# Differential attention scores: two maps as 64-row matmul pairs on the two row groups, three products of parts, pieces of 512 columns

## What is computed

```python
s = einsum('ibhqd,ibhkd->ibhqk', qblk, k) * scale + bias   # i: the map, 0 or 1
s = where(rel >= 0, s, -inf)                               # causal
p = softmax(s, axis=-1)
a = p[0] - lam * p[1]
o = einsum('bhqk,bhkd->bhqd', a, v)
```

## Time and profile before

| | |
|---|---|
| median of 3 runs | 2482.14 us |
| lowest to highest | 2478.25 to 2485.72 us |
| span of the profiled execution | 2482.5 us |
| PE busy | 2290.3 us, 92% |
| DVE, ACT, POOL busy | 56%, 49%, 31% |
| mean granted clock of TensorE | 0.968 |

### The profile page before, as it was taken

How to read it: one execution, slowest core, us unless ns; L and a number is a source line. 1 busy time by engine, 2 the same in 40 slices (tenths; PEclk the granted TensorE clock), 3 DMA queues, 4 the chain that set the end, 5 groups by cost and what they waited for, 6 DMA issues and landing times. The chain is left out here.

```text
span 2482.5 us, 36835 instructions
## 1 busy us (share of the span) xinstructions
PE 2290.3 (92%) x11480; PEld 1838.1 (74%) x11480; DVE 1382.3 (56%) x2806; ACT 1207.9 (49%) x1639; POOL 766.9 (31%) x686
## 2 busy tenths in 40 slices
PE   6999999997999999999979996699999999999980
PEld 5788889996777667766658885577888888788760
DVE  6321221104777777777546776676655565666663
ACT  5111111113777677767644443475554555656653
POOL 0000000003887778777600111222222222222220
PEclk9999999998999999999989997799999999999995
DMA  5433334224553454344036444599877878988957
GB/s 196 161 120 126 114 131 121 62 65 121 134 126 81 100 134 100 81 100 132 18 133 206 133 129 162 203 334 353 285 263 250 273 241 279 314 288 282 325 148 288
DMA packets 207632, 441.51 MB, mean 178 GB/s; under 512 B 19081, under 2 KB 56113, under 8 KB 205490
## 3 DMA queue, kind: packets, MB, share of 16 engines
q1 hardware_dynamic: 188530, 379.46, 46.1%
q0 software_dynamic: 19008, 60.91, 9.8%
HBM read 338.55 MB, written 101.76 MB: 177 GB/s over the span
## 5 line engine op out<-in xcount | busy, mean ns | idle before, releaser
L1495 DVE TENSOR_TENSOR gu_lo<-gu_raw,gu_hi 128x2048 fp32r<-128x2048 f32 x128 | 293.2, 2291 | 124.2 <-issue 86.8
L622 POOL TENSOR_TENSOR p_ring<-p_ring 128x512 f32<-128x512 f32 (+2 forms) x192 | 334.2, 1741 | 16.0
L682 DVE TENSOR_SCALAR_CACHE_REDUCE p_ring<-ps_s 128x512 f32<-128x512 f32 (+6 forms) x352 | 277.0, 791 | 101.6 <-PE ps_s L753 94.3
L647 ACT ACTIVATE p_ring<-p_ring,shift 128x1152 f32<-128x1152 f32 (+15 forms) x256 | 305.8, 1197 | 22.5 <-DVE shift L698 22.5
L790 PE MATMUL ps_o<-aT,v_st 128*128 128x512 f32 (+3 forms) x640 | 285.5, 530 | 0.0
L636 ACT ACTIVATE aT<-ps_t 128x512 f32<-128x512 f32 (+1 forms) x320 | 168.8, 530 | 171.4 <-PE ps_t L775 170.2
L1435 ACT ACTIVATE gu_hi<-gu_raw 128x2048 fp32r (+1 forms) x128 | 237.9, 1915 | 9.5 <-PE ps_g L1572 4.9
L1572 PE MATMUL ps_g<-gu_hi,xT_lo 128*128 128x512 f32 x720 | 235.6, 408 | 7.5 <-DVE xT_lo L1510 7.5
L1572 PE MATMUL ps_g<-gu_lo,xT_hi 128*128 128x512 f32 x720 | 227.8, 398 | 0.0
L1572 PE MATMUL ps_g<-gu_hi,xT_hi 128*128 128x512 f32 x720 | 227.6, 397 | 0.0
L619 POOL TENSOR_SCALAR p_ring<-p_ring,coef 128x512 f32<-128x512 f32 (+2 forms) x192 | 167.7, 873 | 133.7 <-DVE coef L711 131.9
(11 more groups left out here) (217 smaller groups left out, 4358.9 us busy)
## 6 DMA issues: line engine op xcount, KB each, us to landing
gu_raw<-in_moe_w_gate SPq DMA_DIRECT2D x128, 512.0 KB, 8.6
gu_raw<-in_moe_w_up SPq DMA_DIRECT2D x128, 512.0 KB, 9.8
d_raw<-in_moe_w_down SPq DMA_DIRECT2D x64, 1024.0 KB, 7.2
qk<-stage SPq DMA_DIRECT2D x64, 512.0 KB, 2.8
q_first<-qk SPq DMA_DIRECT2D x64, 256.0 KB, 5.0
q_second<-qk SPq DMA_DIRECT2D x64, 256.0 KB, 5.1
w_raw<-in_diff_w_in POOLq DMA_DIRECT2D x12, 1024.0 KB, 6.6
k<-qk SPq DMA_DIRECT2D x8, 1024.0 KB, 12.5
```

Of the source, the lines that this page charges most:

```text
L622: pool.tensor_tensor(p0(r, c0, c1), p0(r, c0, c1), p1(r, c0, c1), ALU.add).then_inc(mixed, 1)
L647: nc.scalar.activation(p, p, ACT.Exp, bias=shift[:, r % 8, m:m + 1], accum_out=sums[:, r % 8, m:m + 1]).then_inc(raised, 1)
L682: ins = nc.vector.tensor_scalar(p(r, k0, k0 + far), ps_s[:, c % 2, 0:far], SCALE, None, ALU.mult, ALU.max, accum_out=top[:, r % 4, m, col: ...
L1495: nc.vector.tensor_tensor(gu_lo[:, j * GC:(j + 1) * GC], raw(half, j), gu_hi[:, j * GC:(j + 1) * GC].bitcast(F32), ALU.subtract).then_inc( ...
```

## The change

- The two maps of a piece are scored together. q's place now holds, for each part, both maps under each other (map 0 in partitions 0 to 63, map 1 in 64 to 127), and k's too. A matmul takes the 64 rows of one map. The six matmuls of a pair of pieces go in the order (low q, high k), (high q, low k), (high q, high k), each for map 0 and then map 1. The product of the two low parts is no longer computed.
- Pieces have at most 512 columns. A row's first piece takes what is over a multiple of 512 (128, 256, 384 or 512), the rest are 512 wide. Pieces of map 0 and 1 alternate in `pieces`: 640 in place of 384, in 320 pairs.
- `ps_s` is two buffers of two maps of 512 columns (one bank each); the pair starts when DVE has taken the pair before the last (`taken >= c - 2`).
- `take` and `peaks` use up to five columns of `top` for a map.
- The loads of q and k are one DMA each; q's has half the bytes. Places in SBUF shrink, with filler tiles that keep the others where they were.
- `slots` are made by the same rule, two pieces at a time.

```diff
 def load_q_quad(eng, scratch, place, h, j, landed):
-    for hl in range(2):
-        for lanes in (slice(0, HALF), slice(HALF, P)):
-            eng.dma_start(place[lanes, hl].bitcast(F32),
-                          scratch["qk"][h, hl, :, j * 512:(j + 1) * 512].rearrange("(m d) t -> d m t", m=2)
-                          ).then_inc(landed, 16)
+    eng.dma_start(place.bitcast(F32), scratch["qk"][h, :, :, j * 512:(j + 1) * 512].rearrange("l p t -> p l t")
+                  ).then_inc(landed, 16)
...
         w = (i + 1) * P
-        for m in range(2):
-            head = WIDE // 2 if w <= 3 * WIDE // 2 else WIDE
-            for k0, n in [(0, w)] if w <= WIDE else [(0, head), (head, w - head)]:
+        k0 = 0
+        while k0 < w:
+            n = (w - k0 - 1) % PIECE + 1
+            for m in range(2):
                 pieces.append((r, m, k0, n))
+            k0 += n
...
-            scored_cost += pieces[c][3] / (2 * P)
-            c += 1
+            scored_cost += pieces[c][3] / P
+            c += 2
...
-        ps_s = ctx.enter_context(nc.psum_tensor("ps_s", [P, 2, WIDE], F32))
+        ps_s = ctx.enter_context(nc.psum_tensor("ps_s", [P, 2, 2, PIECE], F32))
...
                 if far:
-                    col = 0 if not last else 1
-                    ins = nc.vector.tensor_scalar(p(r, k0, k0 + far), ps_s[:, c % 2, 0:far], SCALE, None,
+                    col = 3 - ((i + 1) * P - k0 - n) // PIECE
+                    ins = nc.vector.tensor_scalar(p(r, k0, k0 + far), ps_s[:, c // 2 % 2, m, 0:far], SCALE, None,
                                                   ALU.mult, ALU.max, accum_out=top[:, r % 4, m, col:col + 1])
...
-                if c >= 2:
-
-                    pe.wait_ge(taken, c - 1)
+                if c >= 4:
+
+                    pe.wait_ge(taken, c - 2)
                 a = i % 4
-                for j in range(0, n, 512):
-                    e = min(512, n - j)
-                    for hl in (1, 0):
-                        mm = pe.matmul(ps_s[:, c % 2, j:j + e], q_st[g % 2][:, hl, m, a * P:(a + 1) * P],
-                                       k_st[h % 2][:, m, k0 + j:k0 + j + e], start=hl == 1, stop=hl == 0)
-                mm.then_inc(scored, 1)
+                for k, (ql, kl) in enumerate(((1, 0), (0, 1), (0, 0))):
+                    for m in range(2):
+                        lanes = slice(m * HALF, (m + 1) * HALF)
+                        mm = pe.matmul(ps_s[:, c // 2 % 2, m, 0:n], q_st[g % 2][lanes, ql, a * P:(a + 1) * P],
+                                       k_st[h % 2][lanes, kl, k0:k0 + n], start=k == 0, stop=k == 2)
+                        if k == 2:
+                            mm.then_inc(scored, 1)
...
-                for c in slots[n]:
+                for c in slots[n][::2]:
                     score(c)
```

More of the change, by code:

```diff
@@ L144, in _ @@
             sp.wait_ge(moved, 32)
-            for hl in range(2):
-                sp.dma_start(k0[hl * HALF:(hl + 1) * HALF].bitcast(F32),
-                             scratch["qk"][HEADS, hl].rearrange("(m d) t -> d m t", m=2)).then_inc(k0_in, 16)
+            sp.dma_start(k0[:, :, :].bitcast(F32), scratch["qk"][HEADS].rearrange("l p t -> p l t")).then_inc(k0_in, 16)
             def store_v(b, first):
@@ L159, in _ @@
             sp.wait_ge(filled, QK_FILLS + (VB - 1) * TILES + 1)
-            load_q_quad(sp, scratch, keep["q_first"], 0, FIRST_QUAD, sem("b_q_in0"))
+            load_q_quad(sp, scratch, keep["q_first"][:, :, :], 0, FIRST_QUAD, sem("b_q_in0"))
             sp.dma_start(keep["near_both"][:, 0, :], scratch["near"][0]).then_inc(k0_in, 16)
@@ L397, in attend @@
     WIDE = 1024
+    PIECE = 512
     QUADS = (FIRST_QUAD, 0, 3, 1)
@@ L490, in attend @@
         oT = sb("oT", [P, 512])
-        sb("q_first_place", [P, 2, 2, 512], F32R)
-        q_st = (keep["q_first"], sb("q_second", [P, 2, 2, 512], F32R))
+        sb("q_first_place", [P, 2, 512], F32R)
+        q_st = (keep["q_first"], sb("q_second", [P, 2, 512], F32R))
+        sb("w_rest_place", [P, 2, D])
         sb("near_place", [P, 2, NEAR])
@@ L495, in attend @@
         o_sb = sb("o_sb", [P, 2, 4, P])
-        top = sb("top", [P, 4, 2, 3])
+        top = sb("top", [P, 4, 2, 5])
         shift = sb("shift", [P, 8, 2])
@@ L532, in load_k @@
         def load_k(eng, h):
-            for hl in range(2):
-                eng.dma_start(k_st[h % 2][hl * HALF:(hl + 1) * HALF].bitcast(F32),
-                              scratch["qk"][HEADS + h, hl].rearrange("(m d) t -> d m t", m=2)).then_inc(k_in[h % 2], 16)
+            eng.dma_start(k_st[h % 2][:, :, :].bitcast(F32), scratch["qk"][HEADS + h].rearrange("l p t -> p l t")
+                          ).then_inc(k_in[h % 2], 16)
         def load_near(eng, h):
@@ L548, in load_q @@
             h, j = quads[g]
-            load_q_quad(eng, scratch, q_st[g % 2], h, j, q_in[g % 2])
+            load_q_quad(eng, scratch, q_st[g % 2][:, :, :], h, j, q_in[g % 2])
         @block.sync
@@ L670, in take @@
                     if r % 16 == 0:
-                        dve.wait_ge(k_in[h % 2], 48 * (h // 2 + 1))
+                        dve.wait_ge(k_in[h % 2], 32 * (h // 2 + 1))
                     if p0_frees[r] >= 0:
@@ L685, in take @@
                     ins = nc.vector.tensor_tensor_reduce(
-                        p(r, k0 + far, k0 + n), ps_s[:, c % 2, far:n], near[:, h % 2, NEAR - n_near:NEAR],
-                        SCALE, LOWEST, ALU.add, ALU.max, top[:, r % 4, m, 2:3])
+                        p(r, k0 + far, k0 + n), ps_s[:, c // 2 % 2, m, far:n], near[:, h % 2, NEAR - n_near:NEAR],
+                        SCALE, LOWEST, ALU.add, ALU.max, top[:, r % 4, m, 4:5])
                 ins.then_inc(taken, 1)
@@ L692, in peaks @@
                 i = rows[r][1]
-                first = 0 if i >= 8 else 1 if i >= 2 else 2
+                first = 4 - ((i + 1) * P + PIECE - 1) // PIECE if i >= 2 else 4
                 if r >= 8:
@@ L697, in peaks @@
                 dve.wait_ge(taken, last_piece[r] + 1)
-                nc.vector.tensor_reduce(shift[:, r % 8, :], top[:, r % 4, :, first:3], AX.X, ALU.max,
+                nc.vector.tensor_reduce(shift[:, r % 8, :], top[:, r % 4, :, first:5], AX.X, ALU.max,
                                         negate=True).then_inc(peaked, 1)
@@ L737, in score @@
             def score(c):
-                r, m, k0, n = pieces[c]
+                r, _, k0, n = pieces[c]
                 g, i = rows[r]
@@ L742, in score @@
                     if r % 16 == 0:
-                        pe.wait_ge(k_in[h % 2], 48 * (h // 2 + 1))
+                        pe.wait_ge(k_in[h % 2], 32 * (h // 2 + 1))
                     if r % 4 == 0:
-                        pe.wait_ge(q_in[g % 2], 64 * (g // 2 + 1))
-                if c >= 2:
-                    pe.wait_ge(taken, c - 1)
+                        pe.wait_ge(q_in[g % 2], 16 * (g // 2 + 1))
+                if c >= 4:
+                    pe.wait_ge(taken, c - 2)
                 a = i % 4
-                for j in range(0, n, 512):
-                    e = min(512, n - j)
-                    for hl in (1, 0):
-                        mm = pe.matmul(ps_s[:, c % 2, j:j + e], q_st[g % 2][:, hl, m, a * P:(a + 1) * P],
-                                       k_st[h % 2][:, m, k0 + j:k0 + j + e], start=hl == 1, stop=hl == 0)
-                mm.then_inc(scored, 1)
+                for k, (ql, kl) in enumerate(((1, 0), (0, 1), (0, 0))):
[5 more added lines that the diff above has]
+                            mm.then_inc(scored, 1)
             def ps_t_free(t):
@@ L1707, in build @@
         with nc.sbuf_tensor("hn_place", [P, 2, KC, SEQ], F32):
-            with nc.sbuf_tensor("q_first", [P, 2, 2, 512], F32R) as q_first:
+            with nc.sbuf_tensor("q_first", [P, 2, 512], F32R) as q_first:
                 keep["q_first"] = q_first
-                with nc.sbuf_tensor("w_place", [P, 2, D], F32):
+                with nc.sbuf_tensor("w_place", [P, 3, D], F32):
                     with nc.sbuf_tensor("near_both", [P, 2, 2 * P], F32) as near_both:
```

## The result

The changed kernel takes 2510.72 us (median of 4 runs, 2510.29 to 2512.92) against 2483.57 us before on the same chip: 1.0116 times as long, 95% interval 1.0101 to 1.013. It is 27 us slower where 35 us less was forecast. The time lies in the range given (2425 to 2560 us), by the rival in which PE pays for each change of shape, whose sum began at +22 us. The profiled execution has a span of 2508.7 us.

What follows compares the result with a forecast made beforehand. PE's stream was taken to bound attention: -64 (overlap) + 4 (loads) + 15 (skew) + 12 (DVE) + 5 (start) = -28 us, or -35 us with skew halved, so 2482 - 35 = 2447 us; range 2425 to 2560 us.

Steps and rivals of the forecast that it cites:

- the rival in which PE pays for each change of shape: In attention, PE empties at each of 512 edges, 0.16 to 0.27 us each: +22 to +78 us, 2532 us; chance 0.33.
- What bounds attention: In attention's steady part PE's stream bounds, busy 568.6 of 582 us; the stages before and after count at nothing.
- Prices of matmuls: Score matmuls on PE, start to start: 0.232 us for 512 columns, 0.176 for 384, 0.12 for 256, 0.084 for 128.
- the overlap: In the scores, the two 64-row matmuls of a pair stream at the same time on PE: a gain of 64 us.
- The edges: 512 changes between 128-row and 64-row work on PE in attention, taken at zero for the change itself.
- the nearest row: PE's change from float32 transposes to float32r scores and back, nothing left over: taken as an edge price of zero.
- Skew of the second map: In each of 256 stretches map 1 ends up to 0.06 us behind map 0: +15 us, or half that.
- Weight loads: Doubled weight loads for score matmuls on PE hide except in 128- and 256-column pairs: +4 us, at most 13 us.
- DVE: In attention's steady part PE's 12.3 us of waits on fuller DVE double: +12 us, between 0 and 30.
- third rival: In attention, DVE frees buffers late, PE's waits rise about 60 us: within 7 us of 2482; 0.12 with middling edges.
- the second: The rival that PE empties at each change of shape in attention: range 2495 to 2565 us, chance 0.33.

Runs made afterwards that it cites:

- e6: The changed kernel with all six matmuls of a pair on rows 0 to 63: 2711.72 us, attention 875.6 us against 701 us.
- e2: The changed kernel with each pair of 64-row matmuls replaced by one 128-row matmul over the same columns: 2588 us in all, attention 657 us.
- e3: The changed kernel with each slot's last pair split around the transposes, giving about twice the stretches of 64-row matmuls: 2604.41 us.
- e10: Two-pass 128-row scores in the change's pieces (2480.84 us), with the second pass of both maps put on rows 0 to 63 alone: 2572.86 us.
- e11: The changed kernel with pairs of pieces held back until two are due and scored together, never three: 2507.68 us, ratio to before 1.0108.
- e4: The changed kernel with all three products of map 0 listed first, then all three of map 1: 2510.37 us.

## Why the prediction was wrong

- **What bounds attention** was right: PE's stream. 23.7 of the 27 us come in its stream after slot 0, and the stages outside take next to no part.
- **Prices of matmuls** were right: 0.232 us for 512 columns also fits the 64-row ones (e6), and the overlap was whole. The gain is there, in the stream: 60 us after slot 0, as priced.
- **The edges** are the step that failed: "I take zero for the change itself, as in the nearest row". The nearest row changed the number format between 128-row matmuls, and that says nothing of a change of rows. The zero was also read in a circle, since the 0.232 us come from the same 1.37 us; e2 bears it out without the circle for that kind of change (0.44 + 0.86 + 3 x 0.232 = 2.00 us asked, 1.99 us found). Measured for the change of rows: 0.35 us for a stretch, 0.09 us at each edge and what fits a weight load in the open after each, 84 to 89 us in all. An edge costs 0.17 us, over the 0.08 us from which the rival was to decide, and near the low end given for it (0.16 us). The rival was described rightly and priced in the right range, but too high in the middle (+50 us): its tail of 0.16 us measured 0.09 us, and its load of 0.11 us measured 0.11 us at one edge and 0.06 us at the other. That the time lies in the stated range is owed to this rival, not to the sum behind 2447 us.
  The rule that was cited with it, the Trainium skill, TensorEngine Tiling (Array Packing), Key Properties, that a change of tiling mode drains TensorE, agrees with e3 and e10; the pages name no price. It should have had more than a third of the chances, since a rule of that kind stood against a row that did not test it.
- **Skew of the second map**, +7 to 15 us, does not show: the 0.20 us within a stretch is as long without overlap (e6), so it belongs to the edge, and in the records the second matmul of a pair mostly starts 3 ns behind the first.
- **Weight loads** of narrow pairs, 4 us: 128-column pairs start 0.11 us apart where 0.084 us were taken for one, and 256-column pairs as before, so it is some 2 us. **DVE**, +12 us, did not come (waits 12.8 us against 12.3 us); e2 shows why, since without the edges the waits rise by 29 us, at the end of the 0 to 30 us that were given: half of what the third rival asks stands behind the second.
- **The sum by what was measured**, in attention: -60 us for the overlap after slot 0, +84 us for the edges, +3 us by the first transpose make +27 us, against 26.4 us there and 27 us in the medians. The 84 us are the remainder of this same sum; what stands by itself is the 89 us from one slot's price, the 94 us of e3 and the 98 us of e10.

No version here beats the kernel before. With edges at 0.35 us a stretch, a 512-column pair costs 0.70 + 0.35 us alone and four 128-row passes 0.93 us; two pairs in a stretch cost 1.74 us against 1.86 us, and DVE does not let that through (e11).

## What to carry to other kernels

Two 64-row matmuls on different row groups cost as much as one, but going from 128-row to 64-row work and back costs 0.33 to 0.35 us of PE each time, one and a half matmuls of 512 columns. Pack rows only where a stretch is long against that, or where all the work around it has the same shape. And where no row shows a price, a row of another kind of change is not its nearest neighbour: keep both ends open in the forecast too.

## What the runs showed of the hardware beyond that

**The two row groups do not keep the program's order with each other.** In e4 all matmuls of one group stand ahead of those of the other, and they overlapped as if they alternated (0.73 us against 0.72 us for six of 384 columns), with the third product of both starting within 10 ns in the records.

**TensorE stayed at 1.2 GHz while it was busy with 64-row matmuls on one group.** Before slot 0 nothing but scores runs. PE's busy time and the granted clock (the last three columns are clock, DMA share and GB/s) from 600 to 617 us, in e6, in which all scores are on one row group:

```profile
600.00:617.00 17.00, 17.00 (x49) 0.50 0.10 31
```

In e10, half of whose score matmuls are:

```profile
600.00:617.00 17.00, 16.16 (x35) 0.50 0.33 75
```

And in the kernel before, less busy and with 128 rows:

```profile
600.00:617.00 17.00, 11.52 (x42) 0.90 0.59 141
```

With the change, both groups in use, the same stretch has 0.70 at 10.97 us busy, and e2, with 128 rows, 0.60 at 10.80 us, so a clock below full is nothing special there. What stands out is a clock of 0.50 with PE busy nearly without a pause: from 590 to 629 us PE is busy 38.8 of 39 us in e6 and 37.95 us in e10, all at 0.50. In e6 the starts of 512-column matmuls lie 0.43 us apart there, 1.8 times the price at full clock; in PE's timeline (7.03 - 0.62) / 15, as the last record lasts 0.62 us:

```profile
599.41 7.03 PE L752 MATMUL ps_s<-k,q_first 64*128 64x512 f32 x16
```

It rose after transposes and products had begun to run between the scores: in e6 they begin at 634.1 us, and the clock is 0.75 from 640 to 650 us and 1.00 in the 10 us after; in e10 they begin at 629.4 us, and it is 0.80 from 634 to 640 us and 1.00 from there to 660 us. Whether the rows in use decide it was not tested apart.
